# Causal scores in blocks of four instead of halves: three wide score steps for six narrow ones

## The reference, cut to what matters

```
S_t = diag(exp(log_a_t)) S_{t-1} + k_t v_t^T ;  o_t = S_t^T q_t

b = cumsum(gc, axis=2)                                  # within a chunk
decay = exp(where(causal, b[t] - b[s], -inf))
scores = einsum('bhtd,bhsd,bhtsd->bhts', qc, kc, decay)
o = einsum('bhts,bhsv->bhtv', scores, vc) + einsum('bhtd,bhdv->bhtv', qc * exp(b), S)
S = exp(b_last) * S + einsum('bhsd,bhsv->bhdv', kc * exp(b_last - b), vc)
```

## Time and profile before

| | |
|---|---|
| median of 3 runs | 1036.46 us (1035.76 to 1039.31) |
| profiled execution | 1035.77 us, its span 1033.9 us |
| busy: PE, PEld, DVE, ACT, POOL | 96%, 71%, 58%, 42%, 36% |
| granted TensorE clock, mean | 0.985 |
| chain that ended last | PE 76%, DVE 14%, ACT 4%, DMA 3%, issue 2% |

### The profile page before, as it was taken

How to read it: one execution, slowest core, us unless ns; L and a number is a source line. 1 busy time by engine, 2 the same in 40 slices (tenths; PEclk the granted TensorE clock), 3 DMA queues, 4 the chain that set the end, 5 groups by cost and what they waited for, 6 DMA issues and landing times.

```text
span 1033.9 us, 26901 instructions
## 1 busy us (share of the span) xinstructions
PE 992.6 (96%) x11652; PEld 737.4 (71%) x11652; DVE 594.5 (58%) x1047; ACT 434.0 (42%) x845; POOL 376.0 (36%) x510
## 2 busy tenths in 40 slices
PE   2997899999999999999999999999999999999997
PEld 2867577855886668865887668865887668866783
DVE  4997578635744466535745467445735467335564
ACT  6965454531533335431534325432534325333333
POOL 1224441174305550174305650174305641256200
PEclk9997699999999999999999999999999999999999
DMA  8820432001220013101220013101220013001011
GB/s 309 292 92 3 135 121 61 9 1 42 63 62 1 2 63 65 39 2 42 63 62 1 2 63 62 42 1 42 63 62 2 2 62 59 25 2 42 1 65 44
DMA packets 41527, 56.21 MB, mean 54 GB/s; under 512 B 27793, under 2 KB 28603, under 8 KB 41403
## 3 DMA queue, kind: packets, MB, share of 16 engines
q1 hardware_dynamic: 41411, 54.51, 17.1%
HBM read 38.44 MB, written 9.86 MB: 47 GB/s over the span
## 4 chain that ended last, share of the span: by engine, by line
PE 76%; DVE 14%; ACT 4%; DMA 3%; issue 2%; SPq 1%; POOL 0%; DVEq 0%; ACTq 0%
PE pj L688 37%; PE op L911 15%; PE pj L707 7%; PE sc L786 6%; DVE w_lo L1812 2%; DMA h_lo<-xres 2%; PE m L843 2%; PE m L891 1%; PE sc L931 1%; PE op L931 1%; PE sc L797 1%; DVE A L1928 1%; DVE X L2075 1%; PE pj L883 1%; DVE B L1865 1%
## 5 line engine op out<-in xcount | busy, mean ns | idle before, releaser
L688 PE MATMUL pj<-h_hi,w_hi 128*128 128x256 f16 (+1 forms) x1728 | 211.4, 266 | 0.7
L688 PE MATMUL pj<-h_lo,w_hi 128*128 128x256 f16 (+1 forms) x1728 | 210.4, 265 | 0.0
L688 PE MATMUL pj<-h_hi,w_lo 128*128 128x256 f16 (+1 forms) x1728 | 209.0, 264 | 0.0
L521 POOL TENSOR_TENSOR G<-B 128x256 f32<-128x256 f32 x112 | 78.9, 705 | 290.1 <-DVE B L1865 166.7
L1928 DVE COPY_PREDICATED A<-cu,sc 64x256 f32<-64x256 uint8 x192 | 102.6, 534 | 131.6 <-PE sc L786 129.2
L688 PEld LDWEIGHTS pj<-h_hi,w_hi 128*128 128x128 f16 x1728 | 151.7, 99 | 28.6 <-issue 4.4
L688 PEld LDWEIGHTS pj<-h_lo,w_hi 128*128 128x128 f16 x1728 | 158.7, 99 | 18.2
L688 PEld LDWEIGHTS pj<-h_hi,w_lo 128*128 128x128 f16 x1728 | 158.1, 99 | 17.8
L532 POOL TENSOR_TENSOR G<-G,Q 128x256 f32<-128x256 f32 x112 | 87.7, 783 | 113.9 <-issue 70.0
L1356 ACT ACTIVATE G<-G 128x512 f32<-128x512 f32 x112 | 69.1, 622 | 79.4 <-POOL G L522 79.3
L533 POOL TENSOR_TENSOR G<-G,K 128x256 f32<-128x256 f32 x112 | 92.4, 825 | 0.0
(11 more groups left out here) (289 smaller groups left out, 1357.9 us busy)
## 6 DMA issues: line engine op xcount, KB each, us to landing
xin<-in_x_prompt SPq DMA_DIRECT2D x17, 512.0 KB, 4.4
wo_hi<-in_w_units SPq DMA_DIRECT2D x16, 512.0 KB, 5.5
xres<-in_x_prompt SPq DMA_DIRECT2D x15, 512.0 KB, 3.6
out_y_prompt<-xres SPq DMA_DIRECT2D x14, 512.0 KB, 2.6
wo_lo<-in_w_units SPq DMA_DIRECT2D x12, 512.0 KB, 5.9
xres<-in_w_out SPq DMA_DIRECT2D x8, 256.0 KB, 3.0
gpost<-in_w_out SPq DMA_DIRECT2D x8, 256.0 KB, 4.7
m_hi<-in_state_gla SPq DMA_DIRECT2D x1, 512.0 KB, 8.7
```

Source lines behind the costliest of these rows:

```text
L521: pool.tensor_tensor(Gv[R], Bv[R], mid, ALU.subtract).then_inc(*give(pool, "gs", i, 2 * n + 1))
L688: m = pe.matmul(b[:, j * T:(j + 1) * T], w[:, k, col + 128 * j:col + 128 * j + 128], h[:, k, :], start=(n == 0 and k == 0), stop=(n == 2 a ...
```

## The change

From tile 2 on (`BY_FOUR` = 2, the third tile) level 64 stays, and the six lower levels are replaced by three steps with blocks of w = 16, 4 and 1 tokens (`FOURS`), four blocks to a group of 4w. With three points m in a group, the ends of its blocks 0, 1 and 2, keys of block a take the end of their own block, and queries come in three variants: relative to the end of block 0 for the blocks 1 to 3, of block 1 for 2 and 3, of block 2 for 3, thus 6w queries for 4w tokens. A product has 64 keys x 96 queries. On POOL a step is four subtractions and four products (384, 256, 128 elements for the queries, 384 for the keys), on ACT two exponentials (768 and 384), on TensorE again 16 matmuls (32 records), on DVE three pairs of predicated copies with 384, 256 and 128 elements, one pair for each variant, with a wait on DVE's own last instruction between pairs, since each writes next to the other.

The larger buffers come from two places in turn: the three `G` together (`g_all`), and the `H` buffers of the next tile, which `H_hi` and `H_lo` now share. So POOL waits for the last projection of the tile before, and `turn_x` for the last block-of-one scores of branch 1 of the present tile. The lists of all engines for tiles 2 to 8 are written anew. Where one half projection stood between score steps, two or a whole output piece stand now; but between the block-of-one step of branch 1 and its diagonal there is one.

```diff
-NCF, NCU = 319, 1024
+NCF, NCU = 319, 1312
+FOURS = (None, 16, 4, 1)
+BY_FOUR = 2
 def levels(i):
+    if i >= BY_FOUR:
+        return [0, 1, 2, 3]
     return [5, 6] if i == 0 else [0, 1, 2, 3, 4, 5, 6]
...
+        def g_top(i):
+            free = H[(i + 1) % 2][:, :].bitcast(F32)
+            return G[0], free[:, 1536:2048].rearrange("p (j t) -> p j t", j=2)
+
+        def g_four(i, br, lv):
+            free = H[(i + 1) % 2][:, :].bitcast(F32)
+            t = (g_all[:, :], free)[(lv + br + 1) % 2]
+            return t[:, 0:512].rearrange("p (j t) -> p j t", j=2), t[:, 512:1280].rearrange("p (j t) -> p j t", j=2)
...
             def turn_x(i, c):
-                sp.wait_ge(*filled(i - 2, "c_z"))
+                sp.wait_ge(*at("sc", i - 1, 2 * at_score(i - 1, 1, 3) + 2))
...
+        def four_exponents(i, br, lv):
+            (keys, queries), w, n = g_four(i, br, lv), FOURS[lv], factors_done(i, br, lv) - 4
+            from_, ends = blocks(b_of(i, br), w), blocks(b_of(i, br), w)[:, :, :, w - 1:w]
...
+            for a_ in range(3):
+                pool.tensor_tensor(later(queries, w, a_), from_[:, :, a_ + 1:4],
+                                   ends[:, :, a_:a_ + 1].broadcast_to([128, 128 // w, 3 - a_, w]), ALU.subtract
+                                   ).then_inc(*give(pool, "gs", i, n + a_ + 1))
+            if lv == 1 and br == 0:
+                pool.wait_ge(*at("sc", i, 2 * at_score(i, 0, 0) + 2))
+            pool.tensor_tensor(blocks(keys, w)[:, :, 0:3], ends[:, :, 0:3].broadcast_to([128, 128 // w, 3, w]),
+                               from_[:, :, 0:3], ALU.subtract).then_inc(*give(pool, "gs", i, n + 4))
...
+            if i >= BY_FOUR and 0 < lv < DIAG:
+                keys, queries = g_four(i, br, lv)
+                for c in range(2):
+                    for j in range(2):
+                        for hh in range(2):
+                            for u in range(2):
+                                n, col = 2 * c + u, (2 * c + j) * 128
+                                m = pe.matmul(half(SC[hh], u)[:, col:col + 96], half(keys, hh)[:, j, 64 * n:64 * n + 64],
+                                              half(queries, hh)[:, j, 96 * n:96 * n + 96], start=True, stop=True)
...
+            elif i >= BY_FOUR and lv < DIAG:
+                w = FOURS[lv]
+                for a_ in range(3):
+                    cols = slice((0, 3, 5)[a_] * w, (3, 5, 6)[a_] * w)
+                    if a_:
+                        dve.wait_ge(*own(dve))
+                    for u in range(2):
+                        to = half(A, u)[:, :, 64 * u:64 * u + 64].rearrange("p k (g t) -> p k g t", t=4 * w)
+                        mk = half(masks4, u)[:, 96 * lv - 96:96 * lv].rearrange("p (g t) -> p g t", t=6 * w)
+                        from_ = half(sc, u).rearrange("p (k t) -> p k t", t=128)[:, :, 0:96]
+                        m = dve.copy_predicated(to[:, :, :, (a_ + 1) * w:4 * w],
+                                                mk[:, :, cols].unsqueeze(1).broadcast_to([64, 8, 16 // w, (3 - a_) * w]),
+                                                from_.rearrange("p k (g t) -> p k g t", t=6 * w)[:, :, :, cols])
+                    if a_ < 2:
+                        m.then_inc(*give1(dve, "dve"))
```

On ACT's list of the loop the two changes that the prediction names are these (`gate_in(i - 1, "C")` stands between `level_exp(i, 0, 0)` and `gate_log`):

```diff
                 level_exp(i, 0, 0)
                 gate_in(i - 1, "C")
-                level_exp(i, 0, 1)
                 gate_log(i - 1, "C")
-                level_exp(i, 0, 2)
                 gate_sigmoid(i - 1, "C")
...
                 conv_gate(i)
+                keys_out(i, 1)
                 if i < NT:
                     x_norm(i + 1, 1)
                     x_hi(i + 1, 1)
-                keys_out(i, 1)
                 square(i, 1)
```

More of the change, by code:

```diff
@@ L128, in nth @@
         return k
+    if name in FEWER and i >= BY_FOUR:
+        return FIRST[name] + (BY_FOUR - 1) * SIGNALS[name] + (i - BY_FOUR) * FEWER[name] + k
     return (0 if name in OWN0 else FIRST.get(name, SIGNALS[name])) + (i - 1) * SIGNALS[name] + k
@@ L173, in program @@
         gpost = sb("gpost", [128, D])
-        G = [sb(f"G{n}", [128, 2, TT]) for n in range(3)]
+        g_all = sb("G", [128, 6 * TT])
+        G = [g_all[:, 512 * n:512 * n + 512].rearrange("p (j t) -> p j t", j=2) for n in range(3)]
         A = sb("A", [128, 8, CH])
@@ L363, in split, with blocks, later @@
             return t[:, :, :].rearrange("p j (b w) -> p (j b) w", w=2 * h), TT
+        def blocks(t, w):
+            return t[:, :, :].rearrange("p j (g b t) -> p (j g) b t", b=4, t=w)
+        def later(t, w, a_):
+            return t[:, :, :].rearrange("p j (g b t) -> p (j g) b t", b=6, t=w)[:, :, (0, 3, 5)[a_]:(3, 5, 6)[a_]]
         def pair(t, T):
@@ L516, in exponents @@
                 pool.wait_ge(*at("qt", i, 0))
-            if n >= 3:
+            if i >= BY_FOUR and br:
+                pool.wait_ge(*filled(i - 1, "c_z"))
+            if n >= 3 and i < BY_FOUR:
                 per = len(levels(i))
@@ L1351, in level_exp @@
         def level_exp(i, br, lv):
+            if i >= BY_FOUR and lv > 0:
+                keys, queries = g_four(i, br, lv)
+                for n, v in ((1, queries), (0, blocks(keys, FOURS[lv])[:, :, 0:3])):
+                    act.wait_ge(*at("gs", i, factors_done(i, br, lv) - n))
+                    act.activation(v, v, ACT.Exp, scale=SCALE[br]).then_inc(*give(act, "ge", i, exps_done(i, br, lv) - n))
+                return
             n = at_level(i, br, lv)
@@ L2388, in _ @@
                 gate_abs(i, "B")
+                gate_min(i, "B")
                 if i < NT:
                     alpha_sum(i + 1)
-                gate_min(i, "B")
+                gate(i, "B")
                 normalise(i, 1)
-                gate(i, "B")
                 mix_lo(i, "B")
@@ L2477, in constants @@
         masks[:, 64 * lv:64 * lv + 64] = level_mask(h, CH)
+    fours = np.zeros((128, 3 * 96), np.uint8)
+    for n, w in enumerate(FOURS[1:]):
+        g, a = np.arange(96) // (6 * w), np.array((0, 0, 0, 1, 1, 2))[np.arange(96) // w % 6]
+        fours[:, 96 * n:96 * n + 96] = (p[:, None] % 64 // (4 * w) == g) & (p[:, None] // w % 4 == a)
     masks0 = np.zeros((T0, 4 * 24 + T0), np.uint8)
```

331 lines of the change are left out of this document (177 added, 154 removed).

## The result

The changed kernel took 1045.29 us (median of 4, 1041.97 to 1045.46), the kernel before 1037.03 beside it: a ratio of 1.007, 95% interval 1.0042 to 1.0097. It is slower by 0.7%, where 1033.8 was forecast. The profiled execution took 1041.97, with a span of 1040.2 for 1033.9, 6.3 more.

The account below looks back on a forecast made before the run. TensorE, busy 96%, was taken as the bound. Per tile -2.9 - 0.9 + 1.1 + 1.8 + 0.7 = -0.3, six tiles -1.7, last tile -1.0, together -2.7: 1033.1 profiled, 1033.8 median; range 1016 to 1049.

Parts of the forecast that it names:

- place A: Diagonal of branch 0: TensorE waits 1.1 us per tile for the block-of-one copy, which stands behind `query_min` on DVE.
- the last tile: Last tile: TensorE saves 2.9 us, a wait of 1.9 at branch 0's diagonal takes part back, together -1.0.
- TensorE's saving: Twelve lower steps of 0.71 us become six of 0.93: 2.9 us saved per tile, bounds 4.1 to -0.7.
- R3: Wide products don't overlap in four array corners: a step takes 1.43 us for 0.82, total 1051; chance 0.06.
- The copies: DVE's predicated copies of the block-of-one step: short runs cost double, three pairs take 4.4 us.
- R1: Copies are not late: block-of-one step at 2.6 us, total 1016 (1025 at 3.5); chance 0.25.
- R2: Short runs in `sc` and the mask cost too: total 1046 with the block-of-one copy at 5.3, 1057 at 6.2; chance 0.18.
- R4: POOL, ACT or the x chain 1 us later than walked at A or C: +6 to +7, total 1041; chance 0.06.
- Place B: Diagonal of branch 1: one half projection (2.7 us) stands before it, the copy takes 4.4 plus 0.1; wait of 1.8.
- Place C: Next tile's low-rank product: the chain from branch 1's block-of-one copy takes 19.3 us against TensorE's 18.6; wait of 0.7.
- The waits of before: TensorE's old waits before the second state update (0.46), low-rank product (0.18) and `a_k` (0.25) go: 0.9 per tile.
- What would show it: Signs in the trace: score step 0.82, copies 4.4, diagonal waits 1.1 and 1.8, low-rank 0.7, period within 1 us of 116.7.

Follow-up runs that it names:

- diag_a: Changed kernel with the block-of-one copy of branch 0 ahead of `query_min` on VectorE in tiles 2 to 7; 1037.17 us.
- The run of the three moves: Changed kernel, last tile only: diagonal of branch 0, top step of branch 1 and pooling product each moved later on TensorE; 1040.93 us.
- the second: The changed kernel run once more with nothing edited; median 1043.84 us.
- best1: Changed kernel with block-of-one copy of branch 0 earlier, diagonal of branch 1 later, next tile's input chain earlier on VectorE and ScalarE, three last-tile moves; 1022.32 us.
- best3: best1 with `attend` and transposes one half projection later, `x_norm` further ahead, `keys_out` and `conv_gate` directly behind `x_hi`, `x_lo` directly behind `mix_lo` D; 1017.82 us.

## Why the prediction was wrong

For the middle tiles the mechanism and its places were right: a saving on TensorE, and three places that take it back. The sum was small against its terms (-0.3 per tile out of -3.8 and +3.6), so its sign hung on their sizes. Three of them failed: place A (1.1, measured 1.64 per tile), the last tile (-1.0, measured +1.7, since two of its waits were not in the sum) and the granted clock, put at nothing (1.5).

- **TensorE's saving.** Forecast 2.9 per tile, and measured 2.9: the step is 0.82, and five of the six have a turn of 0.10 ahead of them (575.56 to 576.53 is 0.97, undisturbed 0.87). Rival R3 is refuted.
- **The copies.** 4.4 forecast, 4.45 measured. R1 and R2 are refuted, and with R1 the access granule of the Trainium skill (Vector Engine (DVE) Microarchitecture Reference, section 5.2) for this pattern: the instruction of 256 elements in aligned runs of two took 0.72, as in the earlier trace rows, where runs of eight took 0.43 to 0.44.
- **Place A, the term of the middle tiles that was most mis-sized.** 1.1 forecast, 1.48 and 0.16 measured, 3.2 us over six tiles. All of tile 5 is 1.15 later now (559.41 for 558.26), so "580.6 + 1.2 (0.15 wait, 1.04 ...) + 0.65 + 1.3 + 0.7 = 584.4" reads 585.6 there. GpSimd's factors came as walked (581.86), but `key_exponents`, beside L1990, took 1.28 for 1.04, and `query_min` ended at 585.8; TensorE was there 0.15 sooner. And `attend`, not walked at all, waits 0.16 since `query_decay` (L2062) takes 1.13 beside GpSimd, for 0.68 in diag_a. A small case of R4.
- **Place B.** 1.8 forecast, 1.93 measured. **Place C.** 0.7 forecast, 0.6 on average, but unevenly (0 to 1.73).
- **The waits of before.** 0.9 taken away by the forecast. The timeline names 0.6; the 0.25 ahead of `a_k` is there too, though it prints no wait:

```profile
669.92 1.05 PE L688 MATMUL pj<-h_hi,w_hi 128*128 128x256 f16 x8
```

The eight products before it start at 668.75 and go at 0.87, so 0.30 is lost. With the steps' 2.9 that is -3.8 forecast, and -3.8 measured (116.87 to 113.05 on average).
- **The last tile.** Forecast -1.0, measured +1.7. The 1.9 was right (1.88); the text "-2.9 + 1.9" had no place for the pooling product (1.54) and the tails (0.67), and the saving there is 2.3. VectorE's order in the last tile had not been walked beyond the diagonals. The run of the three moves gave 3.4 back.
- **The clock, in none of the rivals.** 1.5 in the profiled execution, behind the wait of 1.94.

From -1.7 to +3.7 in the stretch: A 3.2, B 0.8, clock 1.5, less 0.6 for C, is 4.9 of 5.4. The other 0.5 is rounding: the terms as printed add to -0.2 per tile, -1.2 for six, where the forecast counts -1.7. With 2.7 for the last tile and 0.8 at the start it makes the 8.9 between the 1033.1 forecast for the profiled execution and its 1041.97. The median of the first set lies 3.3 over that execution, that of the second 1.9. The three slower executions of the first set have a mean clock of 0.978 to 0.979 for 0.982, by which they are an estimated 6 to 8 us longer at half clock; the start alone differs by 7 between the two profiles. How much is the start and how much are more falls behind waits isn't settled.

"What would show it" asked for 1.1 and 1.8 at the diagonals, put down to DVE on `A`, and 0.7 at the low-rank product: the trace has all three, the first longer, and the period is 117.5 on average, inside the 1 us of 116.7 that I allowed (two of the six tiles, 118.2 and 118.3, are outside). An allowance of 1 us a tile is 6 us over the kernel, twice what decides between faster and slower: it could not have told.

## What to carry to other kernels

When an operation gets longer, list every chain of which it is the head, and walk each to where TensorE meets it: 1.7 us on a copy that is made twice a tile cost 3.4 a tile, and taking the wait at B away moved it to the other chain of the same copy. A gain on the bounding engine is kept only when the orders of the others are written again for it; here some ten calls moved were worth 27 us, against a change that by itself lost 8. When a forecast is the small difference of large terms, its chances should say so.

## What the hardware showed unexpectedly

**The granted clock falls behind long waits, not always.** Over the fourteen profiles, between 200 and 1008 us, it fell to 0.50 behind waits of 4.6 us in 6 of 6 cases; behind waits of 1.87 to 2.56 in 10 of 39; behind waits of 1.2 to 1.74 in none of 61. Each fall to 0.50 cost 1.5 to 2.1 us. A wait of 2 us can so cost 4.

**A predicated copy with short gaps costs as much as one without.** 128 elements in single words, 256 in runs of two and 384 in runs of three took 0.72 us each. It isn't the number of runs: before, 256 single words, every second one (the 1.47 of a pair in the earlier trace rows), took the same 0.73, and so did the diagonal's 512 without a gap (0.74). What these five patterns have in common is that they touch 128 groups of four adjacent words of `A`. Copies that touch 96, 64 and 32 of them took 0.59, 0.43 and 0.30. That the group of four is what is paid is read from these patterns alone; no run was made to test it.

**VectorE and GpSimd slow each other.** `x_lo` of a tile's first half, with two inputs in SBUF, took 2.29 and 2.30 where GpSimd's key product ran beside it, and 1.28 in best1 and best3, where it doesn't; there `query_decay` stands beside that product (best1):

```profile
621.08 1.28 DVE L1923 SCALAR_TENSOR_TENSOR xres<-xin,sx,xres 128x1024 f16<-128x1024 f32 x1
...
626.11 1.76 DVE L2062 TENSOR_TENSOR Q<-Q,G 128x512 f32<-128x512 f32 x1
```

It takes 0.68 alone. The Trainium skill (GPSIMD Engine Reference, section 1, Specifications) names VectorE instructions with two SBUF inputs among those that contend with GpSimd; the traces agree.
